# Part of the retention output's low half on GpSimd, and the delta state reads summed in PSUM

## What is computed

```
def token_mixing(xn, ...):                      # per layer, for the prompt and for the 8 samples
    r_q, r_k, r_v, r_g, g_qkv, g_z, g_a, g_b, m_q, gates = split(xn @ w_in)
    o_ret = silu(r_g) * rms_norm(retention(r_q, r_k, r_v, state_ret))
    o_gdn = silu(g_z) * rms_norm(gated_delta(g_qkv, g_a, g_b, state_gdn))   # samples read q^T S and k^T S of their state
    o_mem = cross_attention(m_q, memory)
    merged = sigmoid(gate0) * (o_ret @ w_branch_ret) + sigmoid(gate1) * (o_gdn @ w_branch_gdn) \
           + sigmoid(gate2) * (o_mem @ w_branch_mem)
    return merged @ w_out
```

## Time and profile before

| | us |
|---|---|
| median of three runs | 1864.43 (1863.88 to 1865.13) |
| profiled execution, its own time | 1863.31 |
| its span | 1861.5 |
| PE busy | 1810.6 (97%) |
| weight loads of PE | 1746.6 (94%) |
| DVE busy | 1344.2 (72%) |
| ACT busy | 902.9 (49%) |
| POOL busy | 118.5 (6%) |

### The profile page before, as it was taken

The page is one execution under the profiler, slowest core; times in us unless marked ns, Lnnn a source line. Parts: engine busy times, 40 slices in busy tenths (PEclk is TensorE's granted clock), DMA queues, the critical chain, the costliest instruction groups (busy, mean ns, idle before and its releaser), DMA issues.

```text
span 1861.5 us, 40412 instructions
## 1 busy us (share of the span) xinstructions
PE 1810.6 (97%) x16247; PEld 1746.6 (94%) x16247; DVE 1344.2 (72%) x2096; ACT 902.9 (49%) x1051; POOL 118.5 (6%) x174
## 2 busy tenths in 40 slices
PE   7999999999999999999999999999999899999998
PEld 6999999988989999999999999999889899989998
DVE  6777577787777868877577765868777776887764
ACT  5443354546574254543354434465567545354433
POOL 0000001111210100000000000010112010000000
PEclk9999999999999999999999999999999999999999
DMA  7776666766864656566667766676778465546654
GB/s 231 216 206 192 178 196 221 237 226 216 276 227 139 192 169 220 162 191 168 173 188 212 205 184 198 198 247 201 232 235 283 138 205 170 181 129 189 182 163 133
DMA packets 433619, 368.20 MB, mean 198 GB/s; under 512 B 9395, under 2 KB 411125, under 8 KB 432811
## 3 DMA queue, kind: packets, MB, share of 16 engines
q1 hardware_dynamic: 409560, 276.60, 50.0%
q0 software_dynamic: 23872, 89.03, 14.2%
HBM read 338.90 MB, written 26.69 MB: 196 GB/s over the span
## 4 chain that ended last, share of the span: by engine, by line
PE 71%; DVE 16%; issue 5%; ACT 4%; DMA 2%; DVEq 0%; SPq 0%; ACTq 0%
PE proj L686 46%; PE proj L709 4%; PE proj L704 4%; PE proj L705 4%; DVE wl L1859 3%; ACT wh L1364 2%; PE aux L749 1%; PE proj L660 1%; PE aux L919 1%; PE aux L1141 1%; PE aux L864 1%; PE aux L880 1%; DVE y L2053 1%; DVE x L2054 1%; DMA raw<-w_mem_v 1%
## 5 line engine op out<-in xcount | busy, mean ns | idle before, releaser
L1859 DVE TENSOR_TENSOR wl<-raw,wh 128x2048 fp32r<-128x2048 f32 (+1 forms) x280 | 599.2, 2140 | 193.2 <-ACT wh L1364 167.9
L1364 ACT CAST wh<-raw 128x2048 fp32r<-128x2048 f32 (+1 forms) x280 | 500.3, 1787 | 249.3 <-PE proj L686 105.9
L686 PE MATMUL proj<-xl,wh 128*128 128x264 f32 x2624 | 381.4, 286 | 1.9 <-DVEq L2009 1.3
L686 PE MATMUL proj<-xh,wh 128*128 128x264 f32 x2624 | 380.1, 287 | 0.0
L686 PE MATMUL proj<-xh,wl 128*128 128x264 f32 x2624 | 372.0, 284 | 1.8 <-DVE wl L1859 1.1
L686 PEld LDWEIGHTS proj<-xl,wh 128*128 128x128 f32 x2624 | 341.3, 188 | 15.5 <-issue 13.2
L686 PEld LDWEIGHTS proj<-xh,wl 128*128 128x128 f32 x2624 | 339.0, 188 | 4.2 <-DVE wl L1859 3.9
L686 PEld LDWEIGHTS proj<-xh,wh 128*128 128x128 f32 x2624 | 340.0, 188 | 3.1 <-issue 0.8
L705 PE MATMUL proj<-hl,wh 128*128 128x264 f32 x704 | 173.3, 283 | 0.0
L704 PE MATMUL proj<-hh,wh 128*128 128x264 f32 x704 | 173.0, 283 | 0.0
L1385 ACT ACTIVATE gate<-gate 128x264 f32<-128x264 f32 x88 | 37.4, 425 | 246.2 <-DVEq L1895 246.2
(11 more groups left out here) (477 smaller groups left out, 2271.5 us busy)
## 6 DMA issues: line engine op xcount, KB each, us to landing
raw<-ffn_w_in SPq DMA_DIRECT2D x176, 512.0 KB, 5.1
raw<-w_in SPq DMA_DIRECT2D x80, 1024.0 KB, 5.6
raw<-ffn_w_out SPq DMA_DIRECT2D x64, 704.0 KB, 4.6
sring<-cache_mem_k POOLq DMA_DIRECT2D x32, 512.0 KB, 5.1
sring<-cache_mem_v POOLq DMA_DIRECT2D x32, 512.0 KB, 4.0
out<-sring POOLq DMA_DIRECT2D x32, 512.0 KB, 4.5
sring<-state_gdn POOLq DMA_DIRECT2D x30, 512.0 KB, 5.1
raw<-w_mem_v SPq DMA_DIRECT2D x8, 1024.0 KB, 6.9
```

Of the source, the lines that this page charges most:

```text
L686: mm = pe.matmul(o, w[:, s, k * 256 + t * P:k * 256 + (t + 1) * P], a[:, k, :], **go)
L1364: act.copy(wh[:, slot, 0:size], raw[:, slot, 0:size]).then_inc(hi_done[slot], 1)
L1859: dve.tensor_sub(wl[:, slot, 0:size], raw[:, slot, 0:size], wh[:, slot, 0:size].bitcast(F32)).then_inc(split_done[slot], 1)
```

## The change

Four things. POOL, after its loads of D4 to D7 and E0 to E3, waits for the first `gated_high` and makes the low part of the first four tiles itself; DVE no longer does; PE waits for it (`o_ret_low`) at the end of `x0` group 0. The keys and queries of the samples are laid out in `gqm`, 128 columns for each sample, zero but for the sample's own columns, so that all eight products add up in one PSUM bank (`gd`, bank 1) and DVE copies the sum once (`keep_delta_reads`); PE itself releases the slots of all units but D7. `rn1` moves to banks 2 and 3, which `rn0` holds, and to the second half of group 1; `gQ0` and `gQ1` move to bank 2. `query_part(1)` comes after the `o_ret` signal.

```diff
-              "spt": 2, "gvn0": 0, "rd7": 2, "rS6": 0, "rS7": 2, "rdt": 0, "gqd": 1, "gvn1": 2, "gd0": 1, "rn1": 0, "gd1": 2, "gbr0": 0, "gG0": 3, "gQ0": 1,
-              "gd2": 2, "gbr1": 0, "gG1": 3, "gQ1": 1, "gd3": 2, "gT": 0}
+              "spt": 2, "gvn0": 0, "rd7": 2, "rS6": 0, "rS7": 2, "rdt": 0, "gqd": 1, "gvn1": 2, "gd": 1, "rn1": 2, "gbr0": 0, "gG0": 3, "gQ0": 2,
+              "gbr1": 0, "gG1": 3, "gQ1": 2, "gT": 0}
...
                 for n in range(D_UNIT + SRING, E_UNIT + SRING):
                     unit(l, n)
+                pool.wait_ge(M["rgh"], 2 * l + 1)
+                passed(pool)
+                pool.tensor_tensor(ol[:, 0:4, :], rout[:, 0:4, :], oh[:, 0:4, :].bitcast(F32), ALU.subtract).then_inc(M["o_ret_low"], 1)
...
+                    if (g, t, k) == (1, 1, 1):
+                        retention_sums(1)
                     if (t, k) != (1, 3):
                         return
-                    o = begin(l, f"gd{g}")
-                    for c in range(2):
-                        unit_wait(pe, l, D_UNIT + 2 * g + c)
-                        mm = four_heads(o[:, 0, c * DV:(c + 1) * DV], lambda h: gqw[:, h, :], delta_unit(2 * g + c), start=True, stop=True)
-                    end(mm, f"gd{g}")
+                    o = begin(l, "gd") if g == 0 else aux[:, PLACE["gd"][0]:PLACE["gd"][0] + 1, :]
+                    for b in (2 * g, 2 * g + 1):
+                        slot = unit_wait(pe, l, D_UNIT + b)
+                        mm = four_heads(o[:, 0, 0:DV], lambda h: gqm[:, b * P + h * 32:b * P + (h + 1) * 32], delta_unit(b),
+                                        start=(b == 0), stop=(b == NS - 1))
+                        if b == NS - 1:
+                            end(mm, "gd")
+                        else:
+                            mm.then_inc(unit_used[slot], 1)
...
                         second("rsq", 1)
-                        for s in range(2):
-                            o = begin(l, f"rn{s}")
-                            for hd in range(2):
-                                mm = pe.matmul(o[:, hd, 0:T], ones[:], rsq[:, 2 * s + hd, :], start=True, stop=True)
-                            end(mm, f"rn{s}")
+                        retention_sums(0)
...
                 def inverse_inner(g, t, k):
 
+                    if (g, t, k) == (0, 1, KT - 1):
+                        ready("o_ret_low")
...
+                        if g == 2:
+                            ready("rS_out")
+                            order(dve.memset(gqm[:], 0.0))
...
-                        order(cp(gqw[:].rearrange("p h (c n) -> p c h n", c=2), qkvt[:, 0:8, T - 16:T].rearrange("p (c h) n -> p c h n", c=2)))
+                        last = (NS - 1) * (P + 1)
+                        for c in range(2):
+                            own_columns = gqm[:, 0:last].rearrange("p (b j) -> p b j", j=P + 1)[:, :, NS + 16 * c:P:32]
+                            order.apart(cp(own_columns.rearrange("p b h -> p h b"), qkvt[:, 4 * c:4 * c + 4, SEQ:T - 1]))
+                            order.apart(cp(gqm[:, last + NS + 16 * c::32], qkvt[:, 4 * c:4 * c + 4, T - 1]))
+                        order.wait()
...
-                def read_delta(k):
-
-                    o = take(dve, l, f"gd{k}")[:, 0, :]
-                    for c in range(2):
-                        own_part(accd, o[:, c * DV:(c + 1) * DV], own_row, 2 * k + c)
-                    release(dve, f"gd{k}")
-                    for b in (2 * k, 2 * k + 1):
-                        dve.sem_inc(unit_used[(D_UNIT + b) % SRING], 1)
-                    if k == 3:
-                        tell("reads")
+                def keep_delta_reads():
+
+                    order(cp(accd[:], take(dve, l, "gd")[:, 0, 0:DV]))
+                    release(dve, "gd")
+                    dve.sem_inc(unit_used[(D_UNIT + NS - 1) % SRING], 1)
+                    tell("reads")
...
-                    if g < 3:
-                        read_delta(g)
...
-                        read_delta(3)
-                        query_part(1)
+                        keep_delta_reads()
...
                         gated(1)
-                        gated_low(0)
                         gated_low(1)
                         tell("o_ret")
+                        query_part(1)
```

More of the change, by code:

```diff
@@ L92 @@
             for x in ((f"rd{g}", f"rS{g - 1}") if g else ("svt", "rd0")) + more]
-         + ["gvn1", "gd0", "rn0", "rn1", "gd1", "gbr0", "gG0", "gQ0", "gd2", "gbr1", "gG1", "gQ1", "gd3", "gT"]
+         + ["gvn1", "gd", "rn0", "rn1", "gbr0", "gG0", "gQ0", "gbr1", "gG1", "gQ1", "gT"]
          + [x for g in range(LEVELS)
@@ L99 @@
          + ["p2", "n3", "q3", "p3"])
-ONE_BANK = ("gbr0 gbr1 n1 n2 n3 q1 q2 q3 p1 p2 p3 gaw gab smt spt rks gcs rqd gcol gev gqd gkS gmt svt rdt gdt gT gw0 gw1 mqs0 mqs1 mqs2 mqs3 "
-            + " ".join(f"{n}{k}" for n in ("sp", "rd", "gd", "sv") for k in range(2 * NS)) + " "
+ONE_BANK = ("gbr0 gbr1 n1 n2 n3 q1 q2 q3 p1 p2 p3 gaw gab smt spt rks gcs rqd gcol gev gqd gd gkS gmt svt rdt gdt gT gw0 gw1 mqs0 mqs1 mqs2 mqs3 "
+            + " ".join(f"{n}{k}" for n in ("sp", "rd", "sv") for k in range(2 * NS)) + " "
             + " ".join(f"{n}{s}" for n in ("gG", "gQ") + tuple(f"{n}{g}" for n in ("gy", "gt") for g in range(LEVELS)) for s in range(2)) + " " + " ".join(f"{n}{g}" for n in ("gc", "gu") for g in range(SMALL))).split()
@@ L128 @@
               "spe spr sptd glr_prompt gates_in gsqt conv_p "
-              "x_part sq_half y_half xh_part memhi b1_done o_mem merged rraw rot rvt rkd rvn rvsd rp rS_out rof rsq rlr o_ret "
+              "x_part sq_half y_half xh_part memhi b1_done o_mem merged rraw rot rvt rkd rvn rvsd rp rS_out rof rsq rlr o_ret o_ret_low "
               "conv_s gsq gqr gqk tail cso bcd gexp geb dm dme g_at "
@@ L241, in build @@
         accv, accr, accd = (at(n, a, [P, DV]) for n, a in (("accv", 79424), ("accr", 80448), ("accd", 83584)))
-        gqw = at("gqw", 84608, [P, H, 32])
+        gqm = at("gqm", 67072, [P, NS * P])
         spare = at("spare", 71168, [P, D])
@@ L1072, in _, with retention_sums @@
                 products(l, "x2", (xh, xl), (oh, ol), "mix", branch="o_mem", after=prepare_delta, mid=update_retention, inner=read_retention)
+                def retention_sums(s):
+                    o = begin(l, f"rn{s}")
+                    for hd in range(2):
+                        mm = pe.matmul(o[:, hd, 0:T], ones[:], rsq[:, 2 * s + hd, :], start=True, stop=True)
+                    end(mm, f"rn{s}")
                 def read_delta(g, t, k):
+                    if (g, t, k) == (1, 1, 1):
+                        retention_sums(1)
                     if (t, k) != (1, 3):
                         return
-                    o = begin(l, f"gd{g}")
-                    for c in range(2):
-                        unit_wait(pe, l, D_UNIT + 2 * g + c)
-                        mm = four_heads(o[:, 0, c * DV:(c + 1) * DV], lambda h: gqw[:, h, :], delta_unit(2 * g + c), start=True, stop=True)
-                    end(mm, f"gd{g}")
+                    o = begin(l, "gd") if g == 0 else aux[:, PLACE["gd"][0]:PLACE["gd"][0] + 1, :]
[7 more added lines that the diff above has]
+                            mm.then_inc(unit_used[slot], 1)
                 def blocks(o, left, right):
@@ L2520, in update_delta @@
                 def update_delta(b):
+                    if b == 0:
+                        ready("o_ret_low")
                     if b + 1 < NS:
```

## The result

| | before | changed |
|---|---|---|
| median of five runs, us | 1864.43 (1862.90 to 1867.88) | 1873.69 (1871.67 to 1875.31) |
| profiled execution, its own time | 1863.31 | 1873.33 |
| its span | 1861.5 | 1871.5 |
| granted clock of TensorE over the span | 0.998 | 0.994 |

The changed kernel takes 1.0043 times as long, with a 95% interval of 1.0032 to 1.0055: 9.3 us slower by the medians and 8.0 by the ratio, where 1.8 were forecast, and outside the range.

The account below looks back on a forecast made before the run. PE, busy 97%, was taken to bound the kernel, waiting near x0 on DVE's chain. Chain +0.45 and x2 +0.45 made 0.9 us a layer, 1.8 for both: 1864.43 + 1.8 = 1866.2, range 1862.6 to 1870.9.

Parts of the forecast that it names:

- The wait at `rn1`: PE's new wait in rg until ACT has read rn0, starting DVE's chain later: 1.9 us in each layer.
- The chain's savings: DVE's chain: read_delta(2) goes, -1.34 us; one copy replaces read_delta(3) and query_part(1) ahead of the split, -2.22 us.
- The gap ahead of the last subtraction: After gated(1), DVE idles about 1.2 us for ACT's gated_high(1); dropping gated_low(0) wins only 0.14 us.
- `gkS` behind `query_part(1)`: gkS waits some 2.5 us for query_part(1) to free bank 2, delaying x0 group 1: +2.25 us.
- The memset and the copies in `x2`: Ahead of the chain: 0.15 us at group 3's cso copy and 0.3 for four layout copies, together +0.45 us.
- POOL's own time: POOL's subtraction of 1056 columns taken as two passes, 2.0 us; even 2.9 would cost nothing.
- The overlap of POOL and DVE: POOL's subtraction beside DVE's split and gated(1): price taken as 0, the other end kept for the range.
- Rival A with POOL first: POOL's subtraction holds gated(1): +2.1 us a layer, 1870.4, or 1872.2 with 2.9 us for it; half of 0.36.
- A: POOL's subtraction and DVE's split and gated(1) exclude each other: 1870.4 or 1867.6 by order; chance 0.36.

Follow-up runs that it names:

- rn1_later: dve_low with rn1 moved to k = 4 of half t = 1 instead of k = 1: 1867.93 us, ratio 1.0017 to the kernel before.
- dve_low: The changed kernel without POOL's subtraction, DVE making both low halves after gated(1): 1868.14 us, ratio 1.0014 to the kernel before.
- pool_writes_only: The changed kernel with three POOL memsets of the same tiles replacing its subtraction, DVE then making both low halves: 1869.81 us, ratio 1.0024.
- pool_half: The changed kernel with POOL subtracting only two of its four tiles and DVE the other two: 1870.54 us, ratio 1.0030.
- pool_in_gap: The changed kernel with POOL's subtraction also waiting for gated(1) to end: 1870.32 us, ratio 1.0026.
- pool_alone: The kernel before with only POOL's subtraction of the first four tiles added, banks and delta reads unchanged: 1872.26 us, ratio 1.0035.
- kept_busy_16: The changed kernel with 16 needless matmuls on PE ahead of gkS: 1869.99 us, ratio 1.0026.
- all_moved: gks_free with gc1 in bank 2 and rn1 at k = 4 instead of 1: 1861.13 us, ratio 0.9982.
- memset_on_pool: all_moved with the memset of gqm on POOL in gq instead of on DVE in x2: 1858.91 us, ratio 0.9963.
- gks_free: dve_low with gkS in bank 3 instead of bank 2: 1865.69 us, ratio 1.0007 to the kernel before.

## Why the prediction was wrong

**The wait at `rn1` (1.9): right.** 1.66 us, released by ACT, and the chain starts 2.59 us late, of which 0.6 had come from `x2` (ACT's read at 521.26 instead of 520.63). What `rn1_later` adds is that ACT's work behind the second root stands close behind this delay, by 0.8 us in `dve_low`.

**The chain's savings (-1.34 and -2.22): right.** `decays(1)` is 1.24 late (538.93 against 537.69), so 1.35 were saved; the split is 1.02 early (549.47 against 550.49), so 2.26 more.

**The gap ahead of the last subtraction, and `gkS` behind `query_part(1)`: right.** DVE idles 1.24 us for ACT, where 1.2 was said. `gkS` starts 0.20 after `query_part(1)` (558.55 + 0.69 = 559.24, 559.44), group 1 right behind it. In `dve_low` the wait is 2.49, as worked out.

**The memset and the copies in `x2` (+0.45): the place was wrong and the size near.** I looked for its effect at the `cso` copy of group 3. PE meets it at that of group 2, one group earlier:

```profile
465.91 0.91 DVE L2368 MEMSET gqm<- 128x1024 f32 x1 [0.75 <-DVE kdb L2256]
466.86 1.21 DVE L2369 COPY cso<-aux 27x1024 f32<-27x1024 f32 x1
...
468.18 0.64 PE L922 MATMUL aux<-sring,rqw 128*32 128x256 f32 x8 [1.04 <-DVEq L383]
```

The copy ends at 468.07 and PE, which was ready at 467.14, starts 0.11 later. In the kernel before no wait stands there, which I would have seen with the row of that PE read beside the end of that copy. The four copies of the layout overlap (501.30, 501.39, 501.46, 501.54) and add hardly anything. ACT's operations at the end of `x2` are late by 0.8 us, against 0.45; two layers, 0.7 us in all.

**POOL's own time (2.0): low by 0.4.** Alone it is 2.46 us. Two passes of 0.98, the memset's, would be 1.96.

**The overlap of POOL and DVE, taken as 0: the step that failed.** Rival A with POOL first priced it at 2.1 us for each layer; it measures 3.50 - 1.25 = 2.25. With it the forecast for the start of group 1 is 0.45 + 0.45 + 2.25 = 3.15 late in the first layer; the trace has 560.10 - 556.76 = 3.34. The prediction took 0 since "nothing in these rows holds either"; what the runs show in its place is that whichever of the two is held stands until the other is done. The rival's reason had been that DVE's split and `gated(1)` read two SBUF tensors, as POOL's subtraction does. The runs bear out POOL's side of it: no POOL operation, no stretch (`dve_low`); POOL without reads, no stretch (`pool_writes_only`); half the reading, half the stretch (`pool_half`). That it takes two SBUF inputs on DVE's side isn't shown: in every run all that DVE had beside POOL's subtraction were such operations. The range, too, ended at 1870.9 as "the upper end of A", though the same text had A at 1871.0 and 1872.2 with POOL first. I had put 0.36 on A because no row of the trace of before showed such a conflict. But none could: in the kernel before POOL has nothing but memsets and the issues of transfers. An absence in a trace counts only where the case could have occurred.

The Trainium skill had the rule, in "SBUF — State Buffer", section Who interferes with whom: a DVE instruction with two SBUF inputs contends with a GpSimd instruction that reads SBUF, not with one that only writes. The runs agree in both halves, with 3.50 against 1.25 us and with the 1.25 us beside the memsets; its condition on DVE's inputs no run here tests. Its "GPSIMD Engine Reference", section 3.1, led to an estimate of 2.3 us for the subtraction, and 2.46 was measured. By that page the rival was 1871.0, nearer to the result than the forecast. Its further sentence, that whoever issues first keeps the interface, agrees with the changed kernel, where POOL began 1.45 us into the split and was held, and with `pool_in_gap`, where POOL began 0.93 us ahead of DVE, which was held, and not with `pool_alone`, where the split's row begins 0.47 us ahead of POOL's and it is the split that is held.

**What no step had: the clock.** A wait of 4.64 us (4.59 in the second layer) brings 6.8 us at 1.2 GHz, of which some 4.6 lie behind it, and `kept_busy_16` prices this at 1.95 us on the spot and 1.36 after the next wait. The kernels line up by the length of the wait, though not strictly. With waits of 1.2 us or less in that stretch (`all_moved`, `memset_on_pool`, `kept_busy_16`) and of 1.86 and 1.56 (before) the mean clock of the 20 us is 1.00 in both layers. After 2.49 (`dve_low`) it is 0.91, after 3.22 (`rn1_later`) 0.91, after 3.31 and 3.45 (`pool_writes_only`) 0.91 and 0.83, after 3.58 (`pool_half`) 0.91 in the first layer and 0.83 in the second, after 3.75 (`pool_in_gap`) and 4.64 it is 0.83; `gks_free`, with 2.24 and 2.23, has 0.91 in the first layer and 1.00 in the second. `pool_alone` has two such stretches in its first layer, of 3.4 us each, one behind each of its waits, and group 1's first six matmuls between them are still at the upper level (0.99 us). The first follows a wait of 1.84 us for `gdt` (eight matmuls take 2.11 us), and before, behind a wait of 1.86 at the same place, there is none (eight take 1.23): about the same wait went either way. I had written the longer wait as idle time only.

**The sum again.** For each layer 0.9 as forecast, 0.35 more in `x2`, 2.25 for the exclusion and 1.36 for the clock; 0.24 go off, since `gkS` at the upper clock delays group 1 by 0.36 us (`kept_busy_16`) and not by the 0.60 taken: 4.62, where the two layers show 4.5 and 4.0. The two layers are 8.5 of the 10.0 us between the spans. Why the second shows less, and where the 1.7 us between the layers come from, wasn't traced to a cause and stays open. The clock's term is the least certain of them: by the nets of the table `kept_busy_16` is 2.2 us below the changed kernel in the first layer and only 0.4 in the second, where the stretches show 1.36 and 1.35.

**Where "gets worse" turns.** The forecast called the rest of the change a loss of 1.8 us, and `dve_low` measures 2.6 (0.7 to 4.3 by its interval). Its loss isn't in the delta reads, whose 3.6 us on DVE are saved, but in the bank table: `gkS` behind `gQ1`, `gc1` behind the reader that `query_part(1)` delays, and a memset in a place where DVE had 0.2 us to spare (its copy ended at 466.94, PE's read began at 467.13). With these three moved (and `rn1` with them, whose part in that wasn't tried apart) the delta reads' part of the change is worth 0.37%, and POOL has only the memset.

## What to carry to other kernels

Before work goes from DVE to a GpSimd engine that is idle, ask which operands each side reads. Here a GpSimd operation that reads SBUF cost a DVE chain of two-input operations nearly its whole length, so it would have paid only in a gap of DVE as long as itself, while a memset cost the chain nothing. Where a step's order is moved, go through the bank table for every step that PE's program has behind it, since a wait that is removed by another bank comes up at the next step that shares the old one. And a long wait of PE can cost more than its length: price the matmuls behind it at the lower clock too.

## What was unexpected of the hardware

- Which of the two is held isn't told by the order of the rows' starts alone. POOL's row beginning 1.45 us into DVE's split left the split at 2.29 us and held POOL (3.14 instead of 2.46) and then `gated(1)`; beginning 0.47 us into it, the split took 5.08 us and ended 2.15 behind POOL's end, as if it had done next to nothing before (in the second layer the same, 5.02). What decides between 0.47 and 1.45 wasn't tried, and whether a row's start is the moment at which an engine takes hold of SBUF isn't shown.
- A held operation showed as a longer row and not as idle time, on DVE and on POOL, so busy shares hide it: POOL's busy time rose by 6.4 us in the changed kernel for two subtractions that alone are 4.9.
- A matmul of 128 x 128 by 128 columns in float32, repeated on the same two tiles, took 0.23 us (8.20 / 36; 3.73 / 16), as two instructions of the trace each.
